# A forward pass in split fp32r: weights made stationary in five of six feed-forward groups

## The chip, the cores and the metric

One NeuronCore of a Trainium2 chip runs the whole program. The metric is the device time of one execution in microseconds (us). Its engines are TensorE (PE in the profile, PEld for its weight loads), VectorE (DVE), ScalarE (ACT), GpSimdE (POOL) and SyncE (SP, which issues the weight DMAs).

## The reference

It is a forward pass over 256 tokens (S) of width 1024 (D): four layers (feed-forward, mixer, feed-forward), then two layers (three-branch mixing, cross-attention, feed-forward). So there are ten feed-forwards, all of one form:

```python
def swiglu(h, w_in, w_out):
    gate, up = jnp.split(h @ w_in, 2, axis=-1)
    return (jax.nn.silu(gate) * up) @ w_out

x = x + 0.5 * rms_norm(swiglu(rms_norm(x, g[0]), ff1_w_in[i], ff1_w_out[i]), g[1])
```

`h` is 256x1024, `w_in` is 1024x5632 (2816 columns of gate, 2816 of up), `w_out` is 2816x1024, everything in float32.

## The kernel before

**Products in three passes.** A float32 matrix is kept as two fp32r parts, high (rounded) and low (the rest). `split_mm` multiplies high by high, high by low and low by high, three matmuls into one PSUM bank. Activations stand transposed in `hT.high` and `hT.low` (128 x 8 x 256: `hT[:, k, tokens]`).

**Weights.** SP loads them in chunks of 1 MB (128x2048 a chunk: four blocks of 128 rows by 512 columns) into a ring of nine slots; a chunk uses two slots. `ahead(key)` on ACT copies the high part of the chunk three places further on (L1321), and `ahead(key)` on DVE subtracts to leave the low part in the raw slot (L1819). A chunk's split on ACT waits until PE has finished the chunk four places before it. Where `ahead` stands in an engine's program is where that work is done: each engine works strictly through its own list.

**PSUM.** There are eight banks of 128x512. `Banks.take` gives the next bank of a list and makes PE wait until ACT and DVE have read what was in it. The list `G` is banks 0 to 3, `YB` is 4 to 7, `SB` is 4 and 5, `TB` is 6 and 7, `FRESH` is bank 4.

**A feed-forward** (`ffn`, on PE, ACT and DVE alike) has three parts.

1. `first_rows`: group 0, which is 256 columns of gate and 256 of up side by side in one bank of 512, for token half t = 0 (bank from `FRESH`) and t = 1 (bank from `G`, never bank 0). ACT takes Silu of the left half into `silu`, with the row factor `row_factor_of` (the rms norm's factor of each token) as scale (L1395). DVE multiplies the right half by the factor and by `silu` into `hid_f`, tokens on the partitions (L1951). On DVE the splits of `ahead((st, "first", t))` come ahead of L1951 for the same t.
2. Groups 1 to 5: 512 columns of gate, then 512 of up. Each takes two banks of `G` (t = 0, 1) and two chunks (h = 0, 1, four k-blocks each). The activations are stationary and the weights move, 512 columns a matmul. ACT does Silu on the gate bank (L1405), DVE multiplies the up bank (L1963). Halfway through the gate of group g, `turned_hidden(st, g - 1, YB)` transposes the hidden values of the group before (L1025: 8 transposes, 4 for group 0), and ACT and DVE split them into `hidT.high` (L1295) and `hidT.low` (L1981).
3. `wide_gemm`: the output product, in four banks, from `SB` and `TB`, all taken before its first matmul; chunks of `w_out` in eleven steps. Step n waits for the hidden blocks it needs; those of group 5 are transposed after step 0 (`second`).

Of the kernel before, what the change touches and what calls it, by code (L numbers as in the profile page):

```python
# [16 lines left out]
P = 128  # L17
# [221 lines left out]
def build(nc, w, out, plan, stop=None):  # L239
# [22 lines left out]
    with ExitStack() as ctx:  # L262
# [15 lines left out]
        hT = Split(sb("hT_high", [P, KD, S], F32R), sb("hT_low", [P, KD, S], F32R))  # L278
# [5 lines left out]
        fold = sb("fold", [P, 2, CMP_STRIDE])  # L284
        minus_half = sb("minus_half", [P, 16])
# [20 lines left out]
        hid_f = sc  # L306
        tmp2 = xn[:, 1, 512:1024]
# [405 lines left out]
        def _(pe):  # L713
# [234 lines left out]
            def wide_gemm(st, ckeys, key, src, between=None, second=None):  # L948
# [19 lines left out]
                for n in range(together):  # L968
                    if between and n == 4:
                        between()  # L970
                    if second and n == 1:
                        second()
# [21 lines left out]
            def ffn(st):  # L994
                first_rows(st, [(st, "first", h) for h in range(2)], lambda t: (st, "up", 0, t))
                for g in range(1, GROUPS_F):
                    for kind in ("gate", "up"):
                        banks = [G.take(pe, (st, kind, g, t)) for t in range(NT)]
                        for h in range(2):
# [3 lines left out]
                            for t in range(NT):  # L1003
                                for k in range(4):
                                    ins = split_mm(banks[t][:, :], hT[:, 4 * h + k, t * P:(t + 1) * P], s[:, k, :],
                                                   h == 0 and k == 0, h == 1 and k == 3)
                                if h == 1:
                                    ins.then_inc(matmul_done.sem, matmul_done.next((st, kind, g, t)))
                            if h == 0:
                                ins.then_inc(matmul_done.sem, matmul_done.next((st, kind, g, "half")))  # L1010
                            chunk_end[ckey] = (st, kind, g, 1 if h else "half")
                            if kind == "gate" and h == 0:
                                turned_hidden(st, g - 1, YB)
                wide_gemm(st[0], [(st, "out", m) for m in range(KF // 2)], (st, "y"), hidT, set_up if st == stages[0] else None,
                          lambda: turned_hidden(st, GROUPS_F - 1, G))
# [276 lines left out]
        def _(act):  # L1292
# [95 lines left out]
            def ffn(st):  # L1388
# [8 lines left out]
                for g in range(1, GROUPS_F):  # L1397
                    ahead((st, "gate", g, 0))
                    hidden_high(st, g - 1)
# [402 lines left out]
        def _(dve):  # L1802
# [141 lines left out]
            def ffn(st):  # L1944
# [9 lines left out]
                for g in range(1, GROUPS_F):  # L1954
# [3 lines left out]
                    for h in range(2):  # L1958
                        ahead((st, "up", g, h))
# [545 lines left out]
```

## Time and profile before

| | |
|---|---|
| three timed runs | 3039.13, 3040.71 (median), 3049.1 us |
| the profiled execution | 3042.0 us, its span 3040.3 us |
| instructions | 38290, of them 15499 matmuls |
| moved by DMA | 533 MB, 175 GB/s |

The span runs from the first to the last instruction that the profiler recorded; the 1.7 us between it and the execution's time lie outside. A row's "busy" is the union of its instructions' times. Matmuls overlap in the pipeline, so what one costs is read from the distance between starts, not from its duration. In a timeline row, "start, length, engine line ... xN" merges N instructions that follow each other; brackets hold idle time before the row and who ended it.

### The profile page before, as it was taken

Reading aid. Unit: us, or ns where it says so; the run is one execution under the profiler, and the core shown is the slowest. Engines: PE = TensorE matmul, PEld = TensorE weight load, DVE = VectorE, ACT = ScalarE, POOL = GpSimd, SP = SyncE. Lnnn points to the kernel's source line nnn. Section 1 sums busy time; section 2 is a strip of 40 time slices with the busy share of each in tenths; the row PEclk is TensorE's granted clock in tenths of the full one; section 3 lists DMA queues with packets and bytes.
Section 4 is the critical chain, followed back from the end, with each engine's and each line's share of the span. In section 5 each row is a group of like instructions: output and inputs, shape, how many; then the busy total and the mean of one; then the engine's idle time right before and its main releaser. Section 6 shows DMA issues by size and latency. Waiting matters only on the chain.

```text
span 3040.3 us, 38290 instructions
## 1 busy us (share of the span) xinstructions
PE 2992.0 (98%) x15499; PEld 2526.9 (83%) x15499; DVE 1850.5 (61%) x2322; ACT 1480.4 (49%) x2163; POOL 84.1 (3%) x153
## 2 busy tenths in 40 slices
PE   8999999999999999999999999999999999999999
PEld 6889888888888888888888988897888889788887
DVE  5556655546655546755554665469775547977553
ACT  5445544435544435554443564354655434565542
POOL 0000000000000001000000000010000001000000
PEclk9999999999999999999999999999999999999999
DMA  7564455555555555265555635576244548615453
GB/s 229 186 208 141 161 192 177 194 190 199 183 181 190 190 181 186 84 201 188 193 180 175 219 119 193 179 203 210 84 159 150 190 166 226 200 69 171 152 189 126
DMA packets 302403, 532.98 MB, mean 175 GB/s; under 512 B 31074, under 2 KB 125204, under 8 KB 302228
## 3 DMA queue, kind: packets, MB, share of 16 engines
q1 hardware_dynamic: 288964, 511.63, 51.4%
q10 hardware_dynamic: 13264, 18.90, 1.8%
q8 instruction: 124, 2.03, 0.3%
q14 instruction: 51, 0.42, 0.0%
HBM read 528.33 MB, written 1.11 MB: 174 GB/s over the span
## 4 chain that ended last, share of the span: by engine, by line
PE 89%; DVE 8%; ACT 1%; issue 1%; DMA 1%; ACTq 0%; POOL 0%; SPq 0%; POOLq 0%; DVEq 0%
PE bank L724 85%; DVE sb_arena L2280 3%; DVE sb_parts L1819 2%; PE bank L1025 2%; PE bank L1053 1%; PE bank L805 1%; DMA sb_ring<-in_w_xq_dram 1%; ACT sb_parts L1321 0%; DVE sb_sc L2000 0%; PE bank L788 0%; PE bank L780 0%; ACT sb_sc L1457 0%; DVE sb_prT L2010 0%; POOL sb_rstd L1728 0%; DMA sb_ring<-in_ff_w_in_dram 0%
## 5 line engine op out<-in xcount | busy, mean ns | idle before, releaser
L1819 DVE TENSOR_TENSOR sb_parts<-sb_ring,sb_parts 128x2048 fp32r<-128x2048 f32 x480 | 1097.4, 2290 | 788.8 <-ACT sb_parts L1321 786.5
L724 PE MATMUL bank<-sb_parts,sb_hT_high 128*128 128x512 f32 (+1 forms) x4480 | 1370.0, 392 | 7.0 <-DVE sb_parts L1819 6.7
L1321 ACT ACTIVATE sb_parts<-sb_ring 128x2048 fp32r<-128x2048 f32 x480 | 914.5, 1913 | 790.6 <-PE bank L724 695.8
L724 PEld LDWEIGHTS bank<-sb_parts,sb_hT_high 128*128 128x128 f32 x4480 | 835.7, 188 | 184.4 <-DVE sb_parts L1819 11.0
L724 PE MATMUL bank<-sb_parts,sb_hT_low 128*128 128x512 f32 (+1 forms) x2240 | 853.0, 390 | 0.0
L724 PE MATMUL bank<-sb_parts,sb_hidden_high 128*128 128x512 f32 x1760 | 553.7, 395 | 0.0
L724 PEld LDWEIGHTS bank<-sb_parts,sb_hT_low 128*128 128x128 f32 x2240 | 420.9, 188 | 88.0
L724 PEld LDWEIGHTS bank<-sb_parts,sb_hidden_high 128*128 128x128 f32 x1760 | 328.3, 187 | 80.3 <-issue 0.6
L724 PE MATMUL bank<-sb_parts,sb_hidden_low 128*128 128x512 f32 x880 | 347.0, 394 | 0.0
L724 PE MATMUL bank<-sb_hT_high,sb_parts 128*128 128x256 f32 x1408 | 254.5, 283 | 0.0
L724 PEld LDWEIGHTS bank<-sb_hT_high,sb_parts 128*128 128x128 f32 x1408 | 220.1, 192 | 0.2
L724 PE MATMUL bank<-sb_hT_low,sb_parts 128*128 128x256 f32 x704 | 199.2, 283 | 0.0
L724 PEld LDWEIGHTS bank<-sb_parts,sb_hidden_low 128*128 128x128 f32 x880 | 164.7, 187 | 40.7
L724 PE MATMUL bank<-sb_parts,sb_oT_high 128*128 128x512 f32 (+1 forms) x616 | 177.9, 390 | 0.8 <-ACT sb_oT_high L1295 0.8
L1295 ACT ACTIVATE sb_hidden_high<-bank 128x512 fp32r<-128x512 f32 x110 | 60.4, 597 | 210.4 <-PE bank L1025 210.4
L1981 DVE TENSOR_TENSOR sb_hidden_low<-bank,sb_hidden_high 128x512 fp32r<-128x512 f32 x110 | 71.3, 686 | 107.4 <-ACT sb_hidden_high L1295 107.4
L724 PEld LDWEIGHTS bank<-sb_hT_low,sb_parts 128*128 128x128 f32 x704 | 135.1, 192 | 0.2
L724 PEld LDWEIGHTS bank<-sb_parts,sb_oT_high 128*128 128x128 f32 x616 | 112.6, 188 | 24.9 <-issue 3.0
L1457 ACT ACTIVATE sb_sc<-sb_sc,sb_nmax 128x256 f32<-128x256 f32 (+3 forms) x224 | 95.3, 427 | 73.7 <-DVE sb_nmax L2002 73.6
L1728 POOL TENSOR_TENSOR sb_rstd<-sb_mean_sq,sb_minus_half 128x1 f32<-128x1 f32 (+1 forms) x79 | 49.9, 632 | 2895.7 <-DVE sb_mean_sq L1838 2532.0
L1405 ACT ACTIVATE sb_prT<-bank,sb_rstd 128x512 f32<-128x512 f32 x100 | 69.2, 692 | 116.8 <-PE bank L724 116.8
L724 PE MATMUL bank<-sb_parts,sb_oT_low 128*128 128x512 f32 (+1 forms) x308 | 107.2, 386 | 0.0
(220 smaller groups left out, 2083.8 us busy)
## 6 DMA issues: line engine op xcount, KB each, us to landing
sb_ring<-in_ff_w_in_dram SPq DMA_DIRECT2D x160, 1024.0 KB, 5.2
sb_ring<-in_ff_w_out_dram SPq DMA_DIRECT2D x88, 1024.0 KB, 4.9
sb_ring<-in_w_gate_up_dram SPq DMA_DIRECT2D x40, 1024.0 KB, 5.2
sb_ring<-in_w_in_dram SPq DMA_DIRECT2D x38, 1024.0 KB, 5.2
sb_ring<-in_a_w_qkv_dram SPq DMA_DIRECT2D x24, 1024.0 KB, 5.3
sb_ring<-in_w_down_dram SPq DMA_DIRECT2D x22, 1024.0 KB, 5.0
sb_ring<-in_ff_w_in_dram SPq DMA_DIRECT2D x32, 512.0 KB, 4.8
sb_ring<-in_c_w_qkv_dram SPq DMA_DIRECT2D x12, 1024.0 KB, 5.1
```

The lines of the kernel that those rows point to most:

```text
L724: return nc.tensor.matmul(o, lhsT, rhs, start=start, stop=stop)
L805: ins = nc.tensor.transpose(o, i, ident[:, :])
L1025: ins = nc.tensor.transpose(bank[:, c * S + t * P:c * S + (t + 1) * P], hid_f[:, t, (2 * b + c) * P:(2 * b + c + 1) * P], ident[:, :])
L1053: ins = nc.tensor.transpose(bank[0:n, c:c + P], sc[:, (i - 2) % 3, k0:k0 + n], ident[:, :])
L1295: return nc.scalar.activation(o, i, ACT.Copy, scale=scale)
L1321: nc.scalar.activation(halves(n, slice(0, filled(n))).high, ring[:, raw_in[n], 0:filled(n)], ACT.Copy) \
L1405: nc.scalar.activation(silu[:, t, :], G.of((st, "gate", g, t))[:, :], ACT.Silu, scale=row_factor_of(st, t)) \
L1457: ins = nc.scalar.activation(part_of, part_of, ACT.Exp, bias=nmax[:, i % 3, j:j + 1], accum_out=sums[:, u["t"], u["col"]:u["col"] + 1])
L1728: pool.tensor_tensor(rstd[:, c0:c0 + n], mean_sq[:, c0:c0 + n], minus_half[:, 0:n], ALU.pow) \
L1819: V.tensor_tensor(both.low, ring[:, raw_in[n], 0:filled(n)], both.high.bitcast(F32), ALU.subtract) \
L1981: V.tensor_tensor(hidT.low[:, k:k + 2, :], G.of((st, "hid", g, b))[:, :].rearrange("p (c s) -> p c s", c=2), hidT.high[:, k:k + 2, :].bitc ...
L2280: ins = V.scalar_tensor_tensor(convT[:, c, :], src, wt, convT[:, c, :], ALU.mult, ALU.add)
```

## The change

In groups 1 to 5 of each feed-forward the weights become the stationary side. A bank now holds one block f of 128 hidden columns (on the partitions) and 512 columns: 256 tokens times the high part of x, and beside it 256 tokens times the low part. `hT` is laid out so that one access pattern takes high and low side by side (`hT_parts[:, :, k, :]`, two runs of 256). Per block and k one matmul of 512 columns (high weights) and one of 256 (low weights by high x, onto the left half) are issued; four banks are used for gate (`G`) and four for up (`YB`). ACT copies the right half out (`low_part`), DVE adds the left half to it, multiplies by the row factors, which now lie along the free dimension, and the product with Silu is already in the layout of `hidT`. The row factors are brought into that layout once per feed-forward by a matmul of `ones` with a diagonal (`factors`). Only group 0 is still transposed. `wide_gemm` loses `second`; the number of chunks, their order and their DMAs stay.

```diff
@@ -275,13 +275,15 @@
-        hT = Split(sb("hT_high", [P, KD, S], F32R), sb("hT_low", [P, KD, S], F32R))
+        hT_parts = sb("hT", [P, 2, KD, S], F32R)
+        hT = Split(hT_parts[:, 0], hT_parts[:, 1])
...
+        gate_f, up_f = prT[:, :, :].rearrange("p n (b s) -> p (n b) s", b=2), sc[:, 0:2, :].rearrange("p n (b s) -> p (n b) s", b=2)
+        factors, factor_diag = sc[:, 2, 0:S], sc[:, 2, S:2 * S]
...
@@ -994,25 +996,30 @@
             def ffn(st):
                 first_rows(st, [(st, "first", h) for h in range(2)], lambda t: (st, "up", 0, t))
                 for g in range(1, GROUPS_F):
-                    for kind in ("gate", "up"):
-                        banks = [G.take(pe, (st, kind, g, t)) for t in range(NT)]
+                    for kind, take in (("gate", G), ("up", YB)):
+                        banks = [take.take(pe, (st, kind, g, f)) for f in range(4)]
                         for h in range(2):
                             ckey = (st, kind, g, h)
                             arrived(ckey)
                             s = view(ckey)
-                            for t in range(NT):
+                            for f in range(4):
                                 for k in range(4):
-                                    ins = split_mm(banks[t][:, :], hT[:, 4 * h + k, t * P:(t + 1) * P], s[:, k, :],
-                                                   h == 0 and k == 0, h == 1 and k == 3)
+                                    first, last = h == 0 and k == 0, h == 1 and k == 3
+                                    block = s[:, k, f * P:(f + 1) * P]
+                                    mm(banks[f][:, :], block.high, hT_parts[:, :, 4 * h + k, :], first, False)
+                                    ins = mm(banks[f][:, 0:S], block.low, hT.high[:, 4 * h + k, :], False, last)
                                 if h == 1:
-                                    ins.then_inc(matmul_done.sem, matmul_done.next((st, kind, g, t)))
+                                    ins.then_inc(matmul_done.sem, matmul_done.next((st, kind, g, f)))
                             if h == 0:
                                 ins.then_inc(matmul_done.sem, matmul_done.next((st, kind, g, "half")))
-                            chunk_end[ckey] = (st, kind, g, 1 if h else "half")
-                            if kind == "gate" and h == 0:
-                                turned_hidden(st, g - 1, YB)
-                wide_gemm(st[0], [(st, "out", m) for m in range(KF // 2)], (st, "y"), hidT, set_up if st == stages[0] else None,
-                          lambda: turned_hidden(st, GROUPS_F - 1, G))
+                            chunk_end[ckey] = (st, kind, g, 3 if h else "half")
+                            if (kind, g, h) == ("gate", 1, 0):
+                                turned_hidden(st, 0, YB)
+                                pe.wait_ge(pool_step.sem, pool_step.at("ones"))
+                                pe.wait_ge(dve_step.sem, dve_step.at((st, "factors")))
+                                mm(YB.take(pe, (st, "factors"))[:, 0:S], ones[:, 0:1].broadcast_to([P, P]), factor_diag, True, True) \
+                                    .then_inc(matmul_done.sem, matmul_done.next((st, "factors")))
+                wide_gemm(st[0], [(st, "out", m) for m in range(KF // 2)], (st, "y"), hidT, set_up if st == stages[0] else None)
...
@@ -1396,16 +1403,23 @@
+                    if g == 1:
+                        act.wait_ge(transposed.sem, transposed.at((st, "hid", 0, 0)))
+                        copy(hidT.high[:, 0:2, :], G.of((st, "hid", 0, 0))[:, :].rearrange("p (c s) -> p c s", c=2)) \
+                            .then_inc(act_step.sem, act_step.next((st, "hid", 0, 0)))
+                        act.wait_ge(matmul_done.sem, matmul_done.at((st, "factors")))
+                        copy(factors, G.of((st, "factors"))[:, 0:S]).then_inc(act_read.sem, act_read.next((st, "factors")))
+                    else:
+                        hidden_high(st, g - 1)
                     ahead((st, "gate", g, 1))
-                    for t in range(NT):
-                        act.wait_ge(matmul_done.sem, matmul_done.at((st, "gate", g, t)))
-
-                        act.wait_ge(dve_read.sem, dve_read.at((st, "up", g - 1, t)))
-                        nc.scalar.activation(silu[:, t, :], G.of((st, "gate", g, t))[:, :], ACT.Silu, scale=row_factor_of(st, t)) \
-                            .then_inc(act_read.sem, act_read.next((st, "gate", g, t)))
+                    low_part(st, "gate", g, gate_f)
+                    for b in range(2):
+                        act.wait_ge(dve_step.sem, dve_step.at((st, "gate", g, b)))
+                        pair = gate_f[:, 2 * b:2 * b + 2, :]
+                        nc.scalar.activation(pair, pair, ACT.Silu).then_inc(act_step.sem, act_step.next((st, "silu", g, b)))
                     for h in range(2):
                         ahead((st, "up", g, h))
+                    low_part(st, "up", g, up_f)
...
@@ -1414,12 +1428,25 @@
+            def low_part(st, kind, g, dst):
+
+                for f in range(4):
+                    act.wait_ge(matmul_done.sem, matmul_done.at((st, kind, g, f)))
+                    if g > 1 and kind == "gate":
+                        act.wait_ge(dve_step.sem, dve_step.at((st, "hid", g - 1, f // 2)))
+                    elif g > 1:
+                        act.wait_ge(dve_read.sem, dve_read.at((st, "hid", g - 1, f // 2)))
+                    else:
+                        act.wait_ge(dve_read.sem, dve_read.at((st, "up", 0, NT - 1)))
+                        act.wait_ge(transposed.sem, transposed.at((st, "hid", 0, 0)))
+                    copy(dst[:, f, :], G.of((st, kind, g, f))[:, S:2 * S]).then_inc(act_read.sem, act_read.next((st, kind, g, f)))
+
             def hidden_high(st, g):
-                for b in range(2 if g else 1):
-                    act.wait_ge(transposed.sem, transposed.at((st, "hid", g, b)))
-                    k = 2 * (2 * g - 1 + b) if g else 0
-                    copy(hidT.high[:, k:k + 2, :], G.of((st, "hid", g, b))[:, :].rearrange("p (c s) -> p c s", c=2)) \
+                for b in range(2):
+                    act.wait_ge(dve_step.sem, dve_step.at((st, "hid", g, b)))
+                    k = 2 * (2 * g - 1 + b)
+                    copy(hidT.high[:, k:k + 2, :], up_f[:, 2 * b:2 * b + 2, :]) \
...
@@ -1951,18 +1979,41 @@
+                for t in range(NT):
+                    ins = V.tensor_scalar(factor_diag[:, t * P:(t + 1) * P], ident[:, :], row_factor_of(st, t), None, ALU.mult)
+                ins.then_inc(dve_step.sem, dve_step.next((st, "factors")))
                 for g in range(1, GROUPS_F):
                     ahead((st, "gate", g, 0))
-                    hidden_low(st, g - 1)
+                    if g == 1:
+                        dve.wait_ge(act_step.sem, act_step.at((st, "hid", 0, 0)))
+                        V.tensor_tensor(hidT.low[:, 0:2, :], G.of((st, "hid", 0, 0))[:, :].rearrange("p (c s) -> p c s", c=2),
+                                        hidT.high[:, 0:2, :].bitcast(F32), ALU.subtract) \
+                            .then_inc(dve_read.sem, dve_read.next((st, "hid", 0, 0)))
+                        dve.wait_ge(act_read.sem, act_read.at((st, "factors")))
+                    else:
+                        hidden_low(st, g - 1)
                     ahead((st, "gate", g, 1))
+                    both_factors = factors.unsqueeze(1).broadcast_to([P, 2, S])
+                    for b in range(2):
+                        pair = gate_f[:, 2 * b:2 * b + 2, :]
+                        for f in (2 * b, 2 * b + 1):
+                            dve.wait_ge(act_read.sem, act_read.at((st, "gate", g, f)))
+                            ins = V.tensor_tensor(gate_f[:, f, :], G.of((st, "gate", g, f))[:, 0:S], gate_f[:, f, :], ALU.add)
+                            settle(dve, ins, dve_read, (st, "gate", g, f))
+                        V.tensor_tensor(pair, pair, both_factors, ALU.mult) \
+                            .then_inc(dve_step.sem, dve_step.next((st, "gate", g, b)))
                     for h in range(2):
                         ahead((st, "up", g, h))
-                    for t in range(NT):
-                        dve.wait_ge(act_read.sem, act_read.at((st, "gate", g, t)))
-                        dve.wait_ge(matmul_done.sem, matmul_done.at((st, "up", g, t)))
-                        V.scalar_tensor_tensor(hid_f[:, t, :], G.of((st, "up", g, t))[:, :], row_factor_of(st, t), silu[:, t, :],
-                                               ALU.mult, ALU.mult) \
-                            .then_inc(dve_read.sem, dve_read.next((st, "up", g, t)))
+                    for b in range(2):
+                        pair = up_f[:, 2 * b:2 * b + 2, :]
+                        for f in (2 * b, 2 * b + 1):
+                            dve.wait_ge(act_read.sem, act_read.at((st, "up", g, f)))
+                            ins = V.tensor_tensor(up_f[:, f, :], G.of((st, "up", g, f))[:, 0:S], up_f[:, f, :], ALU.add)
+                            settle(dve, ins, dve_read, (st, "up", g, f))
+                        dve.wait_ge(act_step.sem, act_step.at((st, "silu", g, b)))
+                        step(V.tensor_tensor(pair, pair, both_factors, ALU.mult))
+                        V.tensor_tensor(pair, pair, gate_f[:, 2 * b:2 * b + 2, :], ALU.mult) \
+                            .then_inc(dve_step.sem, dve_step.next((st, "hid", g, b)))
...
@@ -1975,12 +2026,11 @@
+                    k = 2 * (2 * g - 1 + b)
+                    V.tensor_tensor(hidT.low[:, k:k + 2, :], up_f[:, 2 * b:2 * b + 2, :], hidT.high[:, k:k + 2, :].bitcast(F32),
+                                    ALU.subtract).then_inc(dve_read.sem, dve_read.next((st, "hid", g, b)))
```

## Rows read from the trace of the kernel before

**Rows 1.** The page: busy us (share of the span) and instructions of each engine.

```profile
PE 2992.0 (98%) x15499; PEld 2526.9 (83%) x15499; DVE 1850.5 (61%) x2322; ACT 1480.4 (49%) x2163; POOL 84.1 (3%) x153
```

**Rows 2.** The page: shares of the chain that ended last, by engine.

```profile
PE 89%; DVE 8%; ACT 1%; issue 1%; DMA 1%; ACTq 0%; POOL 0%; SPq 0%; POOLq 0%; DVEq 0%
```

**Rows 3.** Windows: groups 1 to 5 of the second feed-forward, busy us of each engine.

```profile
343.60:456.90 113.30, 113.24 (x517) 93.83 (x517) 63.03 (x42) 52.27 (x43) 0.00 (x0) 1.00 0.59 193
```

**Rows 4.** Timeline of PE around eight transposes (start us, length us, ... xcount).

```profile
370.76 0.39 PE L724 MATMUL bank<-sb_parts,sb_hT_low 128*128 128x512 f32 x1
...
371.44 0.39 PE L724 MATMUL bank<-sb_parts,sb_hT_low 128*128 128x512 f32 x1
371.68 1.03 PE L1025 MATMUL bank<-sb_ident,sb_sc 128*128 128x128 f32 x8
...
373.01 0.39 PE L724 MATMUL bank<-sb_parts,sb_hT_low 128*128 128x512 f32 x1
```

**Rows 5.** Groups of PE instructions: busy us, mean ns of one, idle before.

```profile
L1025 PE MATMUL bank<-sb_ident,sb_sc 128*128 128x128 f32 x440 | 58.0, 273 | 0.3
```

**Rows 6.** Timeline of PE in a mixer's projections, weights stationary, 256 columns moving.

```profile
232.82 0.28 PE L724 MATMUL bank<-sb_hT_low,sb_parts 128*128 128x256 f32 x1
...
233.18 0.28 PE L724 MATMUL bank<-sb_hT_low,sb_parts 128*128 128x256 f32 x1
```

**Rows 7.** Timeline of PE in an attention, plain float32, 256 columns moving.

```profile
301.25 1.08 PE L724 MATMUL bank<-sb_arena 128*128 128x256 f32 x4
```

**Rows 8.** Timeline of PE where group 1's gate begins, after a mixer and after a feed-forward.

```profile
343.65 0.70 PE L724 MATMUL bank<-sb_parts,sb_hT_high 128*128 128x512 f32 x2
...
348.95 0.39 PE L724 MATMUL bank<-sb_parts,sb_hT_low 128*128 128x512 f32 x1
349.40 0.63 PE L1025 MATMUL bank<-sb_ident,sb_sc 128*128 128x128 f32 x4
...
985.31 0.70 PE L724 MATMUL bank<-sb_parts,sb_hT_high 128*128 128x512 f32 x2
```

**Rows 9.** Timeline of DVE in the same two places.

```profile
346.61 2.29 DVE L1819 TENSOR_TENSOR sb_parts<-sb_ring,sb_parts 128x2048 fp32r<-128x2048 f32 x1 [0.51 <-ACT sb_parts L1321]
348.82 0.48 DVE L1951 SCALAR_TENSOR_TENSOR sb_sc<-bank,sb_rstd,sb_prT 128x256 f32<-128x256 f32 x1
...
989.88 0.48 DVE L1951 SCALAR_TENSOR_TENSOR sb_sc<-bank,sb_rstd,sb_prT 128x256 f32<-128x256 f32 x1
```

**Rows 10.** Timeline, all engines, at the end of group 5 and the start of `wide_gemm`.

```profile
451.73 1.92 ACT L1321 ACTIVATE sb_parts<-sb_ring 128x2048 fp32r<-128x2048 f32 x1 [3.01 <-PE bank L724]
...
453.68 2.29 DVE L1819 TENSOR_TENSOR sb_parts<-sb_ring,sb_parts 128x2048 fp32r<-128x2048 f32 x1 [2.63 <-ACT sb_parts L1321]
...
455.88 0.75 DVE L1963 SCALAR_TENSOR_TENSOR sb_sc<-bank,sb_rstd,sb_prT 128x512 f32<-128x512 f32 x1
...
456.91 0.63 PE L724 MATMUL bank<-sb_parts,sb_hidden_high 128*128 128x512 f32 x2
```

**Rows 11.** Groups of DVE instructions, shapes apart: busy us, mean ns of one, idle before.

```profile
L1819 DVE TENSOR_TENSOR sb_parts<-sb_ring,sb_parts 128x2048 fp32r<-128x2048 f32 x472 | 1083.5, 2299 | 786.6 <-ACT sb_parts L1321 784.4 <-DVE sb_xn L2320 0.8
...
L1981 DVE TENSOR_TENSOR sb_hidden_low<-bank,sb_hidden_high 128x512 fp32r<-128x512 f32 x110 | 71.3, 686 | 107.4 <-ACT sb_hidden_high L1295 107.4
...
L2210 DVE TENSOR_TENSOR sb_arena<-sb_arena,sb_tmp 128x512 f32<-128x512 f32 x16 | 11.1, 692 | 0.6
...
L1924 DVE TENSOR_TENSOR sb_oT_low<-bank,sb_oT_high 128x256 fp32r<-128x256 f32 x16 | 5.7, 418 | 2.9 <-ACT sb_oT_high L1295 2.9
```

**Rows 12.** Groups of ACT instructions, shapes apart, the same columns.

```profile
L1405 ACT ACTIVATE sb_prT<-bank,sb_rstd 128x512 f32<-128x512 f32 x100 | 69.2, 692 | 116.8 <-PE bank L724 116.8
...
L1295 ACT ACTIVATE sb_arena<-bank 128x256 f32<-128x256 f32 x36 | 13.3, 380 | 31.6 <-PE bank L724 31.6
```

**Rows 13.** Windows: the one fall of the granted clock (the number before DMA's share).

```profile
2672.80:2676.10 3.30, 3.30 (x10) 2.54 (x9) 1.33 (x6) 3.26 (x12) 0.00 (x0) 0.50 0.00 0
```

**Rows 14.** Timeline of PE: the idle time before that fall.

```profile
2669.69 0.88 PE L780 MATMUL bank<-sb_ident,sb_o_rows 128*128 128x128 f32 x6 [1.49 <-DVEq L1824]
```

More of the change, by code:

```diff
@@ L284, in build @@
         fold = sb("fold", [P, 2, CMP_STRIDE])
+        ones = sb("ones", [P, 1])
         minus_half = sb("minus_half", [P, 16])
@@ L946, in tiled_output, with wide_gemm @@
                             512, bank=banks[t][1], between=next_tile(st) if t == NT - 1 else None)
-            def wide_gemm(st, ckeys, key, src, between=None, second=None):
+            def wide_gemm(st, ckeys, key, src, between=None):
                 final = key[1] == "y"
@@ L970, in wide_gemm @@
                         between()
-                    if second and n == 1:
-                        second()
                     wait_for(n)
@@ L1398, in ffn @@
                     ahead((st, "gate", g, 0))
-                    hidden_high(st, g - 1)
-                    ahead((st, "gate", g, 1))
-                    for t in range(NT):
-                        act.wait_ge(matmul_done.sem, matmul_done.at((st, "gate", g, t)))
-                        act.wait_ge(dve_read.sem, dve_read.at((st, "up", g - 1, t)))
-                        nc.scalar.activation(silu[:, t, :], G.of((st, "gate", g, t))[:, :], ACT.Silu, scale=row_factor_of(st, t)) \
-                            .then_inc(act_read.sem, act_read.next((st, "gate", g, t)))
+                    if g == 1:
[6 more added lines that the diff above has]
+                        hidden_high(st, g - 1)
+                    ahead((st, "gate", g, 1))
+                    low_part(st, "gate", g, gate_f)
[3 more added lines that the diff above has]
+                        nc.scalar.activation(pair, pair, ACT.Silu).then_inc(act_step.sem, act_step.next((st, "silu", g, b)))
                     for h in range(2):
                         ahead((st, "up", g, h))
+                    low_part(st, "up", g, up_f)
                 for m in range(KF // 2 - 1):
@@ L1734, in _ @@
             step(pool.memset(minus_half[:, :], -0.5))
+            step(pool.memset(ones[:, :], 1.0), "ones")
             step(pool.iota(tmp2[0:BUCKETS, 0:16], pattern=[[1, 16]], base=0, channel_multiplier=0,
@@ L1976, in hidden_low @@
             def hidden_low(st, g):
-                for b in range(2 if g else 1):
+                for b in range(2):
                     dve.wait_ge(act_step.sem, act_step.at((st, "hid", g, b)))
-                    k = 2 * (2 * g - 1 + b) if g else 0
-                    V.tensor_tensor(hidT.low[:, k:k + 2, :], G.of((st, "hid", g, b))[:, :].rearrange("p (c s) -> p c s", c=2),
-                                    hidT.high[:, k:k + 2, :].bitcast(F32), ALU.subtract) \
-                        .then_inc(dve_read.sem, dve_read.next((st, "hid", g, b)))
+                    k = 2 * (2 * g - 1 + b)
+                    V.tensor_tensor(hidT.low[:, k:k + 2, :], up_f[:, 2 * b:2 * b + 2, :], hidT.high[:, k:k + 2, :].bitcast(F32),
+                                    ALU.subtract).then_inc(dve_read.sem, dve_read.next((st, "hid", g, b)))
             def attention(st, evacuate, tail=None, lead=None):
```

## The prediction

> **What bounds the kernel now.** I read the page first. PE is busy for 2992.0 of 3040.3 us [rows 1], and PE makes up 89% of the chain that ended last [rows 2]. So almost every nanosecond that PE gains or loses in issuing is a nanosecond of the end, and DVE (61%) and ACT (49%) matter only where PE has to wait for them. Next the windows: in groups 1 to 5 of a feed-forward, 113.3 us long, PE is idle for 0.06 us, DVE works 63.0 us and ACT 52.3 us [rows 3]. There is no waiting in that stage for the change to remove. It can win only by giving PE less to do, and it can lose by giving it more or by making it wait. Then the timelines around the transposes, the start of group 1 and the start of `wide_gemm`, since those are the places where the change takes PSUM banks in another way.
>
> All sums are made against the profiled execution (3042.0 us, span 3040.3). The median of the timed runs is 3040.7, so I take 1.3 us off at the end. A difference of under 0.3%, 9 us, is no change for this kernel.
>
> **Removed: transposes.** Three matmuls of 512 columns take 0.68 us from start to start (370.76 to 371.44), so one costs 0.227. With eight transposes in between, the same distance is 1.57 us (371.44 to 373.01) [rows 4]. A set of eight thus costs PE 0.89 us. Five sets a feed-forward and ten feed-forwards make 50 sets, 400 of the 440 instructions of L1025 [rows 5]; the 40 of group 0 stay. **-44.5 us.** The other side of it, their reading by ACT and DVE, is not on PE's path.
>
> **Changed: the shape of the matmuls.** Before, a kind (gate or up) of a group needs 48 matmuls of 512 columns: 48 x 0.227 = 10.88 us. After, it needs 32 of 512 and 32 of 256 columns; the number of columns is the same. The nearest row for the 256 is the mixer's projection, with the same tiles in the same roles (weights stationary, hT moving): three take 0.36 us, one 0.120 [rows 6]. At 2.4 GHz the columns alone are 213.3 and 106.7 ns, so both sizes carry the same 13.3 ns on top. 32 x (0.227 + 0.120) = 11.10 us, 0.213 more, a hundred times (10 feed-forwards, 5 groups, 2 kinds): **+21.3 us**, which is 1600 more matmuls at 13.3 ns. The Trainium skill, TensorE: Matmul & The Clock Gate, section "Wait — 56ns, not 53.3ns?", gives a warm matmul N / 2.4 GHz plus about 2.5 ns. By that page the 1600 would cost 4 us and this part would come out 17 us lower; the rows show 13.3 ns, and the measurement decides.
>
> What no row shows is the moving operand in two runs of 256 (high and low x). From below it costs nothing, as the columns come at one a cycle in either run. From above it costs like two matmuls of 256, 240 ns instead of 227: 3200 x 13.3 ns = 43 us. I take nothing, since the access stays one instruction.
>
> **Added: the row factors.** One plain float32 matmul of 256 columns per feed-forward, at most 0.27 us as four take 1.08 [rows 7], plus the change of kind: **+3 us**. Its diagonal comes right behind L1951 on DVE and is there long before PE asks for it.
>
> **Moved: banks at the start of group 1.** This is the largest term. Before, gate 1 takes two of the four banks of `G`. After, it takes all four, and `take` makes PE wait for each before the first matmul. One of the four is always the bank of `(st, "up", 0, 1)`, which PE has only just filled: t = 1 of `first_rows` takes from `G`, and the next four takes go once around. So PE waits until L1951 for t = 1 has read it. When is that? DVE has splits queued ahead of it: after the mixer, gate 1 begins at 343.65 [rows 8], while DVE runs a split from 346.61 and then L1951 from 348.82 to 349.30 [rows 9], 5.65 us after. Seven feed-forwards, those that follow a mixer, a memory stage or nothing, show 5.64 to 5.66 us. The three that follow a feed-forward show 985.31 to 990.36, 5.05 us [rows 8, 9]. Nothing that DVE or ACT does up to there hangs on gate 1: their splits wait for chunks of `first_rows`. So L1951 ends at the same time as before. PE goes on about 0.10 us after it (349.30 to the transposes at 349.40). 7 x 5.65 + 3 x 5.05 + 10 x 0.10 = 55.7 us. The kernel before pays a little for the same instruction, halfway through the gate: 348.95 to 349.40 where 0.23 is due [rows 8], about 0.2 us in seven of them, which falls away. **+54.3 us.** PE has no idle time later in the stage [rows 3] out of which it could win this back.
>
> **Moved: banks at the start of wide_gemm.** It takes banks 4 to 7 before its first matmul. Before, the up bank of group 5 is in `G`, so these are free. After, up 5 is in `YB`, the same four banks, and the last of them is full at the very end. What is queued on DVE: the split of a chunk, which follows ACT's at half time, ends at 455.97, and L1963 starts at 455.88 [rows 10], 1.03 us before PE's first matmul of `wide_gemm`. In place of L1963 DVE then does, for blocks 0 and 1, two adds of 0.42 and two products of 0.69, and for blocks 2 and 3 two more adds [rows 11]: 4 x 0.42 + 2 x 0.69 = 3.06 us, and some 0.15 in dependences. It is done at 459.1, PE goes on at 459.2 instead of 456.91, 2.3 us; each half now lasts 0.1 longer and the rest starts as much earlier against its end, so 2.1. The bound from below is ACT's copy of the last block and one add, 0.38 + 0.42 plus the hand-overs, 1.0 us [rows 11, 12]; from above DVE late by one more split, 4.4 us. **+21 us.**
>
> **DVE and ACT otherwise.** Per group DVE had four splits, two L1981 and two L1963, 9.2 + 1.4 + 1.5 = 12.1 us. After: 9.2 + 1.4 + eight adds (3.4) + six products of 0.69 (4.1) = 18.1 us of 22.2 [rows 11]. ACT gains eight copies of 0.38, 3.0 us [rows 12], and gets to about 13. Both stay under PE. Splits are queued three chunks ahead, 16 us before PE needs them, which covers that gate's adds now stand ahead of two of them; without that cover a late split would stop PE for 2.3 us.
>
> **Clock.** The granted clock fell once, to 0.50, that is 1.2 GHz, for over 3.3 us [rows 13], shortly after PE had been idle for 1.49 us and had run small matmuls [rows 14]. At half rate 3.4 us lose 1.7. A wait of over 5 us ten times over invites the same. Part of the low time lies in the wait itself; I take 1.2 us each, **+12 us**, between nothing and 27 (two falls in most places). The Trainium skill, TensorE: Matmul & The Clock Gate, section "HAM oscillation — how this bites in real kernels", describes kernels that lose their clock in each long wait; by that page every one of the ten waits would cost the clock, and this trace shows only the one fall.
>
> **Sum.** -44.5 + 21.3 + 3 + 54.3 + 21 + 12 = +67.1. 3042.0 + 67.1 - 1.3 = 3108 us, slower by 2.2%.
>
> **Rivals.**
> - *The bank of group 0 is free in time* (PE does not wait at gate 1, only at `wide_gemm`). For it: DVE's end of L1951 comes from splits whose place could move. Against it: those lie ahead of L1951 in the list, unchanged. -44.5 + 21.3 + 3 - 1.4 + 21 = -0.6: 3040 us, no change. 0.05.
> - *The other side: faster.* Banks cost nothing at all, because DVE and ACT have read each bank before PE returns; only PE's own work counts: -44.5 + 21.3 + 3 - 1.4 = -21.6, 3019 us. It decides if both waits together stay under 2 us a feed-forward. Against it stands the end of L1951, 5 us past gate 1. 0.07.
> - *Two runs of 256 cost like two matmuls*: 3108 + 43 = 3151 us. For it: no row has such an access. Against: the pattern is still one instruction, and the 13.3 ns come once for each instruction in both sizes [rows 4, 6]. 0.07.
> - *DVE becomes the bound.* With 18.1 us of 22.2 it has 4 to spare a group; if broadcast or in-place products cost double (3.4 us for five, then waits in turn), it reaches 22 and the order of its list makes PE wait 1 to 2 us a group: 50 x 1.5 = 75, 3183 us. 0.04.
> - *The forecast*, both waits: 0.77.
>
> **Range.** The forecast's own: without the clock's 12 and with the short second wait (1.0 instead of 2.1) it is 3108 - 12 - 11 = 3085; with 15 more for the clock and 25 for the second wait being late it is 3148. It holds most of its 0.77, and the rival at 3151 lies at its edge, so 3084 to 3152. Faster 0.07, same 0.06, slower 0.87.
>
> **What the profile after would show.** L1025's row has x40. PE has idle time ended by DVE's L1951 at the first gate matmul, ten times, some 5.4 us each, and ended by DVE's add of block 3 at the first matmul of `wide_gemm`, some 2 us. A pair of 512 and 256 columns takes 0.347 us. The granted clock shows falls behind gate 1's start. The prediction is wrong if PE starts gate 1 without a wait (then L1951's bank is not among the four), if the pair takes more than 0.36, or if PE waits for splits inside the groups.

## The result, and the profile after

The changed kernel takes 3139.0 us (median of 5 runs, 3136.4 to 3141.8), the kernel before 3040.7. The ratio is 1.032, with a 95% interval of 1.0309 to 1.0332. The forecast was 3108 us in a range of 3084 to 3152: the direction and both waits came as described, and the size fell 31 us short, 20 us of it on the clock. The profiled execution took 3136.4 us, 94.4 more than that of before.

The page gives the busy us of each engine (share of the span) and its instructions; it answers to [rows 1]:

```profile
PE 3011.3 (96%) x16719; PEld 2591.0 (83%) x16719; DVE 2135.1 (68%) x2942; ACT 1618.3 (52%) x2573; POOL 84.0 (3%) x154
```

PE has 19 us more busy time, though 400 transposes are gone, and stands still for 123 us of its span instead of 48. The groups of PE instructions say where. Their last column is idle time and who ended it:

```profile
L728 PE MATMUL bank<-sb_hT,sb_parts 128*128 128x512 f32 (+1 forms) x8512 | 1394.9, 326 | 56.5 <-DVE sb_sc L1979 56.5
L728 PE MATMUL bank<-sb_parts,sb_hidden_high 128*128 128x512 f32 x1760 | 563.0, 401 | 21.1 <-DVE sb_sc L2011 21.1
...
L1032 PE MATMUL bank<-sb_ident,sb_sc 128*128 128x128 f32 x40 | 6.0, 272 | 0.0
```

Two waits are there which the kernel before did not have: 56.5 us for L1979, the product of group 0 (L1951 before), and 21.1 us for L2011, the adds of up 5. The transposes are down to 40 [rows 5].

The first wait, timeline of PE and then of DVE at the second feed-forward, as in [rows 8] and [rows 9]:

```profile
352.77 1.52 PE L728 MATMUL bank<-sb_parts,sb_hT 128*128 128x512 f32 x6
360.08 1.41 PE L728 MATMUL bank<-sb_hT,sb_parts 128*128 128x512 f32 x3 [5.79 <-DVE sb_sc L1979]
```

```profile
357.14 2.29 DVE L1847 TENSOR_TENSOR sb_parts<-sb_ring,sb_parts 128x2048 fp32r<-128x2048 f32 x1 [0.49 <-ACT sb_parts L1328]
359.35 0.48 DVE L1979 SCALAR_TENSOR_TENSOR sb_sc<-bank,sb_rstd,sb_prT 128x256 f32<-128x256 f32 x1
```

PE has nothing to do from 354.3, while DVE still splits a chunk that nobody needs yet; the product behind it ends at 359.83 and PE starts at 360.08. The second wait, at the end of group 5 of the same feed-forward, again PE and then DVE, as in [rows 10]:

```profile
472.69 1.55 PE L728 MATMUL bank<-sb_hT,sb_parts 128*128 128x512 f32 x8
476.43 0.71 PE L728 MATMUL bank<-sb_parts,sb_hidden_high 128*128 128x512 f32 x2 [2.19 <-DVE sb_sc L2011]
```

```profile
470.74 2.29 DVE L1847 TENSOR_TENSOR sb_parts<-sb_ring,sb_parts 128x2048 fp32r<-128x2048 f32 x1 [0.67 <-ACT sb_parts L1328]
472.95 0.88 DVE L2011 TENSOR_TENSOR sb_sc<-bank,sb_sc 128x256 f32<-128x256 f32 x2
473.86 0.69 DVE L2014 TENSOR_TENSOR sb_sc<-sb_sc 128x512 f32<-128x512 f32 x1
474.59 0.69 DVE L2015 TENSOR_TENSOR sb_sc<-sb_sc,sb_prT 128x512 f32<-128x512 f32 x1
475.20 0.88 DVE L2011 TENSOR_TENSOR sb_sc<-bank,sb_sc 128x256 f32<-128x256 f32 x2
```

Split, two adds, two products, two adds, as the forecast had it; the last add ends at 476.08. What follows each wait is seen in windows of the same feed-forward. A row gives the window and its length, then busy us (instructions) of PE, PEld, DVE, ACT and POOL, then the granted clock (1.00 is 2.4 GHz, 0.50 is 1.2 GHz), DMA's share and GB/s:

```profile
360.00:364.50 4.50, 4.42 (x14) 3.77 (x15) 2.42 (x3) 0.00 (x0) 0.00 (x0) 0.50 0.00 0
364.60:473.90 109.30, 109.30 (x633) 96.40 (x632) 81.18 (x93) 60.72 (x78) 0.00 (x0) 1.00 0.57 183
477.30:480.60 3.30, 3.30 (x9) 2.61 (x8) 3.30 (x4) 0.63 (x1) 0.00 (x0) 0.50 0.36 145
480.70:540.00 59.30, 59.30 (x260) 47.78 (x258) 24.64 (x18) 19.71 (x17) 0.55 (x1) 1.00 0.49 160
```

PE comes back to work at 1.2 GHz for 4.5 us, and again for 3.3 us. Such a stretch at 1.2 GHz is called a fall below. Between the two waits (second line) PE is never idle: DVE works 81.2 us of 109.3, 74%, and no split comes late.

### The profile page after: what moved, and what is told of

The parts are those of the page before. It is cut to its first block, busy times and chain, and to the rows that moved or that the text cites. A ratio compares the mean times of both kernels' runs of the same rounds, so it can differ in the third digit from the quotient of the medians.

```text
span 3134.6 us, 42537 instructions
## 1 busy us (share of the span) xinstructions
PE 3011.3 (96%) x16719; PEld 2591.0 (83%) x16719; DVE 2135.1 (68%) x2942; ACT 1618.3 (52%) x2573; POOL 84.0 (3%) x154
## 4 chain that ended last, share of the span: by engine, by line
PE 82%; DVE 10%; ACT 4%; issue 3%; DMA 1%; ACTq 0%; POOL 0%; SPq 0%; POOLq 0%; DVEq 0%
PE bank L728 80%; DVE sb_parts L1847 3%; DVE sb_arena L2330 3%; ACT sb_parts L1328 2%; PE bank L1060 1%; ACT sb_hT L1302 1%; DVE sb_sc L2011 1%; PE bank L809 0%; DVE sb_sc L2050 0%; PE bank L792 0%; POOL sb_rstd L1755 0%; ACTq L1583 0%; PE bank L784 0%; DMA sb_ring<-in_w_xq_dram 0%; ACT sb_sc L1484 0%
## 5 line engine op out<-in xcount | busy, mean ns | idle before, releaser
L728 PE MATMUL bank<-sb_hT,sb_parts 128*128 128x512 f32 (+1 forms) x8512 | 1394.9, 326 | 56.5 <-DVE sb_sc L1979 56.5
L728 PEld LDWEIGHTS bank<-sb_hT,sb_parts 128*128 128x128 f32 x8512 | 1246.2, 191 | 203.8 <-DVE sb_sc L1979 60.4
L728 PE MATMUL bank<-sb_parts,sb_hidden_high 128*128 128x512 f32 x1760 | 563.0, 401 | 21.1 <-DVE sb_sc L2011 21.1
L728 PE MATMUL bank<-sb_parts,sb_hT 128*128 128x512 f32 (+1 forms) x1920 | 453.2, 394 | 5.7 <-DVE sb_parts L1847 5.2
L728 PEld LDWEIGHTS bank<-sb_parts,sb_hT 128*128 128x128 f32 x1920 | 360.7, 190 | 83.9 <-DVE sb_parts L1847 9.5
L1302 ACT ACTIVATE sb_prT<-bank 128x256 f32<-128x256 f32 (+1 forms) x252 | 106.3, 422 | 138.1 <-PE bank L728 124.7
L1302 ACT ACTIVATE sb_sc<-bank 128x256 f32<-128x256 f32 x210 | 79.1, 379 | 123.8 <-PE bank L728 123.6
L1966 DVE SCALAR_TENSOR_TENSOR sb_hT<-bank,sb_gT,sb_hT 128x128 fp32r<-128x128 f32 x256 | 69.1, 345 | 56.1 <-ACT sb_hT L1302 56.1
L1302 ACT ACTIVATE sb_hT<-bank,sb_gT 128x128 fp32r<-128x128 f32 (+1 forms) x272 | 75.5, 390 | 57.8 <-PE bank L809 40.2
L2330 DVE SCALAR_TENSOR_TENSOR sb_arena<-sb_arena,sb_convwT 128x256 f32<-128x256 f32 x240 | 97.3, 489 | 0.1
L728 PE MATMUL bank<-sb_arena 128*128 128x128 f32 (+6 forms) x506 | 93.5, 318 | 0.0
```

The lines of the kernel that those rows point to most:

```text
L728: return nc.tensor.matmul(o, lhsT, rhs, start=start, stop=stop)
L1302: return nc.scalar.activation(o, i, ACT.Copy, scale=scale)
L1966: ins = V.scalar_tensor_tensor(d.low, turned_norm(n, t, kt), gain(kt), d.high.bitcast(F32), ALU.mult, ALU.subtract)
L2330: ins = V.scalar_tensor_tensor(convT[:, c, :], src, wt, convT[:, c, :], ALU.mult, ALU.add)
```

## The experiments

Ten runs. All but one (e4_again) are compared with the kernel before, timed on the same chip; the chips of different runs can differ. Edits are against the changed kernel unless a line says otherwise, and `...` marks lines left out.

**PE kept busy in the waits** (e1_fill).

```diff
                 first_rows(st, [(st, "first", h) for h in range(2)], lambda t: (st, "up", 0, t))
+                fill((st, "fill", 0), YB, 22)
...
+                fill((st, "fill", 1), G, 8)
                 wide_gemm(...)
+
+            def fill(key, banks, n):
+
+                bank = banks.take(pe, key)
+                for i in range(n):
+                    mm(bank[:, :], hT.high[:, 0, 0:P], hT_parts[:, :, i % KD, :], i == 0, i == n - 1)
```

> The changed kernel with PE kept busy in both waits: 22 needless matmuls of 512 columns (5.0 us) before the banks of group 1's gate are taken, and 8 (1.8 us) before those of wide_gemm. They fill time in which PE waited anyway. Theory A, the falls of the granted clock follow from the waits and cost 32 us: no falls behind the two places, and 3139 - 32 = 3107 us (3098 to 3116). Rival B, the falls come from the new mix of 512 and 256 columns: they stay where they are, 3139 us. Rival C, the wait is not idle time but has room to shrink: 3139 + up to 68 us for 300 matmuls.

Measured: 3118.2 us (3116.8 to 3119.6), 21 us less with 300 matmuls more. The mean granted clock rose from 0.985 to 0.997. The changed kernel's trace holds 18 falls (one at the very end of the program not counted): ten at gate 1, six at `wide_gemm`, two elsewhere. Here 5 are left: the two elsewhere, in the last two layers, and three in the fill ahead of gate 1, none behind gate 1 or at `wide_gemm`. In the fill the edit had a flaw: in four feed-forwards it took the bank of group 0's first half and waited 2.5 us for it itself, and so ended after the wait that it was meant to fill. Timeline of PE in two of the four, and a window of the second one's fill:

```profile
823.94 5.27 PE L728 MATMUL bank<-sb_hT 128*128 128x512 f32 x22 [2.50 <-DVE sb_sc L1987]
829.05 2.15 PE L728 MATMUL bank<-sb_hT,sb_parts 128*128 128x512 f32 x11
...
1860.50 6.59 PE L728 MATMUL bank<-sb_hT 128*128 128x512 f32 x22 [2.53 <-DVE sb_sc L1987]
1866.92 1.45 PE L728 MATMUL bank<-sb_hT,sb_parts 128*128 128x512 f32 x7
```

```profile
1860.40:1866.90 6.50, 6.40 (x22) 5.22 (x23) 5.28 (x5) 2.58 (x3) 0.00 (x0) 0.77 0.34 130
```

In the first of them DVE's product had ended at 826.98, so PE could have started gate 1 at about 827.2; it did at 829.05, 1.8 us late. In the other three the fill's own wait brought a fall, the fill ran in part at 1.2 GHz (the window's mean is 0.77), and gate 1 came 3.1 to 3.4 us late. That is 11.8 us in the four. It is why the time lies 2 us above the expected 3098 to 3116. Without it the kernel would be at 3106 us, 33 below the changed kernel, where theory A has 32: theory A stands, rivals B and C are out, and a wait costs more than its length.

**Gate banks taken late** (e2_late).

```diff
-                        banks = [take.take(pe, (st, kind, g, f)) for f in range(4)]
+                        banks = [] if kind == "gate" else [take.take(pe, (st, kind, g, f)) for f in range(4)]
...
                             for f in range(4):
+                                if len(banks) == f:
+                                    banks.append(take.take(pe, (st, kind, g, f)))
```

> The changed kernel, gate banks taken one by one, each before its own block's first matmul; the bank of group 0's second half comes fourth. Theory A, only that bank is waited for: PE works 3 x 1.39 = 4.2 us of the 5.9 first, so 42 us less, and the falls behind gate 1 (20 of the 32 us) go as well: 3139 - 62 = 3077 us (3065 to 3090). Rival B, PE waits at gate 1 for something that all four blocks need, such as a weight split: no change, 3139 us. The waits at wide_gemm stay at 2.3 us.

Measured: 3078.0 us (3076.2 to 3081.2). PE in the second feed-forward:

```profile
347.65 4.47 PE L728 MATMUL bank<-sb_hT,sb_parts 128*128 128x512 f32 x24
353.50 0.82 PE L728 MATMUL bank<-sb_hT,sb_parts 128*128 128x512 f32 x3 [1.38 <-DVE sb_sc L1981]
```

Twenty-four matmuls, three blocks, run at once, and only the fourth waits: it is that one bank, as theory A has it. No fall is left behind gate 1.

**Banks exchanged** (e3_swap).

```diff
-                    for kind, take in (("gate", G), ("up", YB)):
+                    for kind, take in (("gate", YB), ("up", G)):
...
-                                turned_hidden(st, 0, YB)
+                                turned_hidden(st, 0, G)
...
-                                mm(YB.take(pe, (st, "factors"))[:, 0:S], ...
+                                mm(G.take(pe, (st, "factors"))[:, 0:S], ...
```

> The changed kernel with the banks exchanged: gate in banks 4 to 7, up in 0 to 3 (the transposes of group 0 and the factors in 0 to 3 too), all four still taken at once. Theory A: at gate 1 the newest bank is now that of group 0's first half, read 3.2 us earlier, so the wait falls from 5.9 to about 2.8 us; at wide_gemm the last readers of banks 4 to 7 are those of gate 5, long done, so that wait is gone. 3139 - 31 - 23, and 10 to 25 less for the clock: 3065 us (3055 to 3078). Rival B, the second wait is for hidden values or splits and not for banks: it stays, about 3100 us.

Measured: 3066.9 us (3065.2 to 3072.3). Who waited for whom, PE's only large row:

```profile
PE bank L728 <- DVE sb_sc L1979: 25.1, 10, 2.7
```

2.5 us each at gate 1, now for the first half's product, and nothing at `wide_gemm`. Six of the ten waits at gate 1 still brought a fall. Rival B is out: PE needed neither hidden values nor splits there, only banks.

**Both** (e4_swap_late): the two edits above and, before group 1, an order that puts the bank of group 0's first half last (it is bank 4, and bank 6 in the last two layers).

```diff
                 first_rows(st, [(st, "first", h) for h in range(2)], lambda t: (st, "up", 0, t))
+                YB.n = 3 if st[0] == "ff3" else 1
```

> Exchange and late taking together, with the order of banks set so that group 0's first half comes fourth. Theory A: neither wait is left and no clock falls follow, so only PE's own work differs from the kernel before: -44.5 + 21.3 + 3 gives -20, the trace of after shows -18, and the 0.2 us wait halfway through gate 1 is back: 3024 us, 0.994 to 0.995 of before. Rival B, once the banks are free, the longer list on DVE (68% busy) makes PE wait for splits in its place: 3040 us or more.

Measured: 3038.0 us (ten runs, 3033.1 to 3045.7), 0.9987 of before (0.9977 to 0.9998). No DVE row holds up PE at gate 1, in groups 1 to 5 or at `wide_gemm`, and no clock falls there. It is 14 us over theory A's number, and not for rival B's reason. Windows of the second and the fourth feed-forward show it (PE's instructions in brackets):

```profile
356.00:455.00 99.00, 99.00 (x573) 87.30 (x572) 76.87 (x88) 56.67 (x71) 0.00 (x0) 1.00 0.58 190
806.00:905.00 99.00, 99.00 (x563) 85.87 (x561) 75.01 (x87) 56.05 (x70) 0.00 (x0) 1.00 0.57 184
```

In the same 99 us, at the same clock and with PE never idle, the one issues 573 matmuls and the other 563. The distances between starts are 346.7 ns a pair in four of the feed-forwards and 353.3 in six, from end to end of groups 1 to 5. A feed-forward has 320 pairs: 320 x 6.67 ns = 2.13 us each, 12.8 in all. Without them the profiled execution (3037.3) would be at 3024.5.

**The same once more** (e4_again), a single execution.

> The kernel of e4_swap_late once more. If the slower pace of some feed-forwards is fixed by the program (addresses, ring slots), the same six are slow (counted from 0: 0, 3, 5, 7, 8, 9). If it is a matter of each run, another set is slow, and the time lies between 3024 us (none) and 3046 us (all ten).

Measured: 3041.3 us. The same two windows:

```profile
356.00:455.00 99.00, 99.00 (x562) 85.81 (x562) 75.25 (x88) 55.77 (x70) 0.00 (x0) 1.00 0.56 181
806.00:905.00 99.00, 99.00 (x563) 85.81 (x562) 76.19 (x88) 54.63 (x71) 0.00 (x0) 1.00 0.56 183
```

The second feed-forward was fast and is slow. The slow ones are 0, 1, 3, 5, 6 and 8 now, and were 0, 3, 5, 7, 8 and 9: the program alone does not decide it. The two profiles are of two chips, so they leave open whether the chip or the single execution does. The times speak for the execution: on one chip and at the same mean granted clock of 0.998, two executions of e8_one_run below took 3037.6 and 3046.5 us, while those of e7_grouped, which has one pace, took 3033.7 and 3035.6. No second profile on one chip shows it directly.

**DVE's and ACT's queue** (e5_order), in `ffn` of both engines, here DVE:

```diff
                 for t in range(NT):
-                    ahead((st, "first", t))
+                    if t == 0:
+                        ahead((st, "first", t))
                     dve.wait_ge(act_read.sem, act_read.at((st, "up", 0, t)))
...
+                ahead((st, "first", 1))
                 for t in range(NT):
                     ins = V.tensor_scalar(factor_diag...
```

> The changed kernel, banks as they are, but on ACT and DVE the split of ahead(first, 1) comes behind Silu and product of group 0's second half instead of ahead of them. Theory A, the length of the wait at gate 1 is set by what is queued on DVE ahead of the product: it ends about 2.8 us earlier after a mixer and 2.2 us after a feed-forward, 26 us in all, and 10 to 20 us of clock come back with it: 3098 us (3088 to 3108). Rival B, the product waits for its Silu or its factor and not for DVE's turn: 3139 us.

Measured: 3107.3 us (3106.0 to 3111.7). Who waited for whom:

```profile
PE bank L728 <- DVE sb_sc L1982: 30.5, 10, 3.2
PE bank L728 <- DVE sb_sc L2015: 20.9, 10, 2.2
```

The first wait fell from 56.5 to 30.5 us, the 26 that were expected, so the queue sets its length: theory A. The clock gave back less than expected: the steps of the granted clock hold 44 us of work at 1.2 GHz in the feed-forwards instead of 61, which is 8 us of time, and five instead of three feed-forwards ran at the slower pace (4 us).

**The wait alone, in the kernel before** (e6_before_wait), an edit of the kernel before:

```diff
                         banks = [G.take(pe, (st, kind, g, t)) for t in range(NT)]
+                        if (kind, g) == ("gate", 1):
+                            pe.wait_ge(dve_read.sem, dve_read.at((st, "up", 0, 1)))
```

> The kernel before with one thing added: PE waits at the start of gate 1 for the read of group 0's second half, as the changed kernel has to. Theory A, the wait and the clock falls behind it have nothing to do with the new matmuls: 3041 + 56 for the wait + 12 to 20 for the clock: 3115 us (3105 to 3122). Rival B, in the old form the stage has slack to make the wait good, or the clock holds: 3097 us or less.

Measured: 3119.4 us (3116.4 to 3123.4), ratio 1.0261 (1.0247 to 1.0275). Who waited for whom:

```profile
PE bank L724 <- DVE sb_sc L1953: 56.4, 10, 5.9
```

56.4 us of waiting, the changed kernel's 56.5, with every matmul as before. Theory A: 79 us of time come from it, and the 22 above the wait are 43.7 us of work at 1.2 GHz, halved. This one wait is four fifths of the change's loss.

**Four of 512, then four of 256** (e7_grouped), against e4_swap_late:

```diff
                                 for k in range(4):
-                                    first, last = h == 0 and k == 0, h == 1 and k == 3
-                                    block = s[:, k, f * P:(f + 1) * P]
-                                    mm(banks[f][:, :], block.high, hT_parts[:, :, 4 * h + k, :], first, False)
-                                    ins = mm(banks[f][:, 0:S], block.low, hT.high[:, 4 * h + k, :], False, last)
+                                    mm(banks[f][:, :], s[:, k, f * P:(f + 1) * P].high, hT_parts[:, :, 4 * h + k, :], h == 0 and k == 0, False)
+                                for k in range(4):
+                                    ins = mm(banks[f][:, 0:S], s[:, k, f * P:(f + 1) * P].low, hT.high[:, 4 * h + k, :], False, h == 1 and k == 3)
```

> As e4_swap_late, but within a block the four matmuls of 512 columns come first and then the four of 256, instead of in turns. In e4_swap_late six of the ten feed-forwards ran at 353.3 ns a pair instead of 346.7, which is 12.8 us. Theory A, the slower pace comes from the taking of turns between the two lengths: all ten run at the fast pace, 3024 us. Rival B, it is a state of the stage into which any stream of this kind can fall: some feed-forwards stay slow, 3028 to 3040 us.

Measured: 3034.6 us (eleven runs, 3032.8 to 3039.5), ratio 0.9982 (0.9973 to 0.9990). Neither theory as it was put. The second feed-forward's window:

```profile
356.00:455.00 99.00, 99.00 (x567) 86.56 (x566) 75.72 (x85) 56.08 (x70) 0.00 (x0) 1.00 0.59 191
```

567 lies between 563 and 573, and all ten feed-forwards last the same, 113.2 to 113.4 us from gate 1 to `wide_gemm` (112.0 or 114.15 in e4_swap_late). The chance has gone out of it, but at a pace in the middle: from start to start a 512 takes 233.6 ns ahead of another 512 and 228.4 ahead of a 256, and a 256 takes 118.5.

**High and low x in one run** (e8_one_run against e4_swap_late, e9_one_run_grouped against e7_grouped):

```diff
-        hT_parts = sb("hT", [P, 2, KD, S], F32R)
-        hT = Split(hT_parts[:, 0], hT_parts[:, 1])
+        hT_parts = sb("hT", [P, KD, 2, S], F32R)
+        hT = Split(hT_parts[:, :, 0], hT_parts[:, :, 1])
...
-        vm = latent_kv[:, 0, 4 * S:KD * S].rearrange("p (t n) -> p t n", t=NT)
+        vm = latent_kv[:, 1, 0:4 * S].rearrange("p (t n) -> p t n", t=NT)
...
-                                    mm(banks[f][:, :], block.high, hT_parts[:, :, 4 * h + k, :], first, False)
+                                    mm(banks[f][:, :], block.high, hT_parts[:, 4 * h + k, :, :], first, False)
```

This is e8_one_run; e9_one_run_grouped changes the operand in the same way in e7_grouped's matmul. (`vm` is another stage's operand; it lies in the memory of `hT` and moves with its layout.)

> As e4_swap_late, but high and low x of a k-block lie next to each other in SBUF (hT as 8 x 2 x 256), so that the moving operand of the 512-column matmul is one run and not two runs of 256 that lie 8 KB apart. Theory A, the slower pace (353.3 ns a pair) comes from the two runs: all ten feed-forwards at 346.7, 3024 us. Rival B, the layout is not it: a few feed-forwards stay slow by chance, 3033 to 3046 us.

> As e7_grouped (four of 512, then four of 256), with the same layout in one run. In e7_grouped the 512-column matmuls ran at 233.6 ns, 7 more than the 226.7 of the kernel before, in all ten feed-forwards. Theory A, that is the price of the two runs: 226.7 and 120, 3024 us. Rival B, it is not: 233.6 again, 3035 us.

Measured: 3038.6 us (3033.7 to 3046.5) and 3036.1 us (3034.1 to 3039.9), 0.9993 (0.9984 to 1.0002) and 0.9982 (0.9973 to 0.9991) of before. In the profiled execution of the first all ten feed-forwards ran slow (561 in the window of 99 us), and that execution took 3046.5 us, which is the 3046 forecast for ten. In the second the window holds 567 again. Rival B in both: the two runs of 256 cost nothing.

## Why the prediction was right, and where its sizes were off

- **Transposes and matmuls.** The pair costs 346.7 ns as forecast from [rows 4, 6], and the two runs nothing. By the rule of N / 2.4 GHz plus 2.5 ns (the Trainium skill, TensorE: Matmul & The Clock Gate, section "Wait — 56ns, not 53.3ns?") it would be an estimated 325 ns; the trace disagrees, as [rows 6] did. e4_swap_late less its slow pace (3024.5) is 17.5 us under the profiled execution of before, against -20.2 forecast for what PE has to do; 1.7 us of the rest are one more fall, in a stretch of matmuls outside the feed-forwards. So the change does save PE that much. The runs show this sum and the pair; the 44.5 us of the transposes were not tested alone. What the forecast lacked is the second pace: 353.3 ns in three feed-forwards of the profiled execution, +6.4 us.
- **The wait at gate 1.** Forecast +54.3. The distance from group 0's last matmul to gate 1 grew by 57.3 us over the ten, less the 1.4 that fell away halfway: +55.9. DVE's product ended where [rows 9] had put it, and e2_late, e5_order and e6_before_wait show bank, queue and price each by itself.
- **The wait at wide_gemm.** Forecast +21. Measured +22.7 (23.9 us from start to start over the ten, less 0.12 each). e3_swap takes it away by an exchange of banks alone.
- **DVE and ACT as cover.** Right: DVE is 74% busy in the window above, where 18.1 of 22.2 us a group, 82%, was forecast, and no matmul inside the groups waits for it or for ACT.
- **The clock.** This term was mis-sized: +12 forecast, "between nothing and 27", about +32 measured. The steps of the granted clock hold 40.7 us of PE's work behind gate 1, 20.5 us behind `wide_gemm` and 3.4 us more than before elsewhere, all at half rate: 64.6 / 2. The forecast took 1.2 us for each wait at gate 1. The trace has nine falls of 6.8 us and one of 3.4 there, of which about 4 us each lie in work and cost 2. And the forecast counted nothing for the 2 us waits, yet six of ten brought a fall of 3.4 us. The row from which I could have known was there: [rows 14] shows a fall after only 1.49 us of idle time. The Trainium skill, TensorE: Matmul & The Clock Gate, section "HAM oscillation — how this bites in real kernels", was nearer than I let it be: by that rule each long wait costs the clock, and the trace agrees for all ten waits at gate 1.

The sum of the parts as measured: 55.9 + 22.7 + 32.3 = 110.9, so that 94.4 leaves -16.5 for PE's own work, where -20.2 + 6.4 = -13.8 would be due. Some 3 us are not placed; stretches outside the feed-forwards differ by as much between executions.

That 3139 still lies in the stated range of 3084 to 3152 is in part luck. The upper end kept 15 us more for the clock and 25 for a late second wait. The clock took 20, the second pace 6 for which nothing was kept, and the second wait, which came on time, left its 25 unused.

## What to carry to other kernels

When a change needs more PSUM banks at once, walk the list of banks back to the last writer of each and look up when its reader ends in the trace before: the engine that reads it may be late for reasons that have nothing to do with it, here a weight split that was queued ahead. Taking the banks one by one, the newest last, and keeping the last group out of the banks that the next stage takes at once, cost nothing and gave back 101 us, more than the 98 that the change had lost. Price a wait of PE in a dense kernel at its length plus half of the time that the work behind it runs at 1.2 GHz, here 22 us on 56.

## What the runs showed that was not expected

- **Two paces at one clock.** With weights stationary and matmuls of 512 and 256 columns in turns, a whole feed-forward runs at 346.7 or at 353.3 ns a pair. Which of them comes differs between two executions of one program (e4_swap_late and e4_again), and it is part of the spread of e4_swap_late's times, 3033 to 3046 us; falls of the clock are another part. Grouping the two sizes gave one pace between them, and the layout of the operand changed nothing. What sets the pace stays open. In the kernel before, stationary `hidT` in `wide_gemm` runs at 233.3 ns (three in 0.70 us below), where stationary `hT` runs at 226.7 [rows 4]. So the form before has two paces as well, but the same one for each stage in all ten feed-forwards:

```profile
456.91 0.63 PE L724 MATMUL bank<-sb_parts,sb_hidden_high 128*128 128x512 f32 x2
457.38 0.40 PE L724 MATMUL bank<-sb_parts,sb_hidden_low 128*128 128x512 f32 x1
457.61 0.63 PE L724 MATMUL bank<-sb_parts,sb_hidden_high 128*128 128x512 f32 x2
```

- **Waits of some 2 us can be enough for the clock.** Behind `wide_gemm`'s wait of 2.1 to 2.5 us, in the middle of dense matmuls, the clock fell to 1.2 GHz in six of ten places; e2_late, where the first wait is cut to 1.4 us, shows it in eight of ten, e5_order, with the same wait, in only two. What decides between them stays open.
- **The best of the versions** are e7_grouped and e9_one_run_grouped, both 0.18% under the kernel before (interval 0.10% to 0.27% for the first); that of e4_swap_late, 0.02% to 0.23%, overlaps. All of it is within what I called no change. Of the 17.5 us that the change saves PE at the better pace, 4.1 ns a pair in 3200 pairs, 13 us, go to the middle pace.
